# RWKV scan: b with U and k with V in opposite halves of the partitions, products over 128 rows, tokens turned 128 wide

## The reference, cut to what matters

```python
def rwkv7_scan(r, w_log, k, v, kk, a, s0):
    def step(s, inp):
        r_t, wl_t, k_t, v_t, kk_t, a_t = inp
        s = (s * jnp.exp(wl_t)[:, :, None, :]
             - jnp.einsum('bhvk,bhk->bhv', s, kk_t)[..., None] * (kk_t * a_t)[:, :, None, :]
             + v_t[..., None] * k_t[:, :, None, :])
        return s, jnp.einsum('bhvk,bhk->bhv', s, r_t)
```

## Time and profile before

| What | Value |
|---|---|
| Time, median of 3 runs | 4886.89 us (4883.68 to 4888.92) |
| The profiled execution's own time | 4901.24 us |
| Its span | 4899.6 us |
| Granted clock of PE over the span | 0.895 |
| PE busy, matmuls | 3998.6 us (82%) |
| DVE, ACT, POOL busy | 2176.6 (44%), 1063.4 (22%), 848.4 us (17%) |
| RWKV scan, from 1009 to 1618 us of the span | 609 us |
| PE busy in the scan | 444.58 us |

### The profile page before, as it was taken

The page is one execution under the profiler, slowest core; times in us unless marked ns, Lnnn a source line. Parts: engine busy times, 40 slices in busy tenths (PEclk is TensorE's granted clock), DMA queues, the critical chain, the costliest instruction groups (busy, mean ns, idle before and its releaser), DMA issues. The chain is left out here.

```text
span 4899.6 us, 92546 instructions
## 1 busy us (share of the span) xinstructions
PE 3998.6 (82%) x37777; PEld 3630.9 (74%) x37777; DVE 2176.6 (44%) x3758; ACT 1063.4 (22%) x1753; POOL 848.4 (17%) x636
## 2 busy tenths in 40 slices
PE   6999676357777788468999999899398289999998
PEld 4999232156666677158999999799377189999998
DVE  3333334233333354245655565500354437555555
ACT  3111233612222343222200010201243313010001
POOL 2222000000000332020222222122011111222221
PEclk8999888679888899679999999999677599999999
DMA  3222555321111221221111111122133411111111
GB/s 128 91 91 73 184 200 174 143 71 52 44 55 42 79 71 53 101 64 31 37 48 43 38 37 41 55 86 79 39 113 100 134 33 40 40 38 44 47 43 60
DMA packets 439455, 360.46 MB, mean 74 GB/s; under 512 B 63220, under 2 KB 417709, under 8 KB 436621
## 3 DMA queue, kind: packets, MB, share of 16 engines
q1 hardware_dynamic: 427729, 287.07, 19.3%
q0 software_dynamic: 10304, 60.98, 3.1%
q10 hardware_dynamic: 1152, 8.39, 0.4%
HBM read 270.45 MB, written 85.92 MB: 73 GB/s over the span
## 5 line engine op out<-in xcount | busy, mean ns | idle before, releaser
L91 POOL TENSOR_TENSOR ffn_w_lower<-ffn_w,ffn_w_upper 128x1024 fp32r<-128x1024 f32 x164 | 393.2, 2398 | 1359.1 <-DVE ffn_w_upper L86 1359.1
L931 DVE SCALAR_TENSOR_TENSOR rstd<-u_tile,ffn_taps,rstd 128x945 f32<-128x945 f32 (+3 forms) x440 | 490.6, 1115 | 85.2 <-ACT rstd L878 71.3
L99 PE MATMUL ffn_ps<-HU,ffn_w_upper 128*128 128x384 f32 x2112 | 481.9, 335 | 29.0 <-DVE ffn_w_lower L91 25.7
L99 PE MATMUL ffn_ps<-HL,ffn_w_upper 128*128 128x384 f32 x2112 | 481.1, 335 | 0.0
L99 PE MATMUL ffn_ps<-HU,ffn_w_lower 128*128 128x384 f32 x2112 | 480.7, 335 | 0.0
L99 PEld LDWEIGHTS ffn_ps<-HU,ffn_w_upper 128*128 128x128 f32 x2112 | 377.1, 188 | 31.8 <-issue 29.2
L99 PEld LDWEIGHTS ffn_ps<-HL,ffn_w_upper 128*128 128x128 f32 x2112 | 377.9, 189 | 0.0
L99 PEld LDWEIGHTS ffn_ps<-HU,ffn_w_lower 128*128 128x128 f32 x2112 | 377.8, 188 | 0.0
L99 PE MATMUL ffn_out_ps<-g_upper,ffn_w_upper 128*128 128x384 f32 x1056 | 355.5, 337 | 22.9 <-DVE g_lower L91 14.5
L99 PE MATMUL ffn_out_ps<-g_lower,ffn_w_upper 128*128 128x384 f32 x1056 | 354.4, 336 | 0.0
L99 PE MATMUL ffn_out_ps<-g_upper,ffn_w_lower 128*128 128x384 f32 x1056 | 354.4, 336 | 0.0
(11 more groups left out here) (468 smaller groups left out, 6588.3 us busy)
## 6 DMA issues: line engine op xcount, KB each, us to landing
ffn_w<-in_ffn_w_in_dram SPq DMA_DIRECT2D x88, 512.0 KB
ada_w<-in_ada_w_dram SPq DMA_DIRECT2D x40, 1024.0 KB, 6.1
rwkv_units<-unit_rows POOLq DMA_DIRECT2D x8, 2304.0 KB, 9.2
un<-rwkv_units SPq DMA_DIRECT2D x36, 512.0 KB, 4.3
z_even<-z_tile POOLq DMA_DIRECT2D x31, 576.0 KB, 3.1
in_w<-in_ab_w_in_dram SPq DMA_DIRECT2D x31, 512.0 KB
gun<-gdn_units SPq DMA_DIRECT2D x72, 192.0 KB, 3.6
z_odd<-z_tile POOLq DMA_DIRECT2D x24, 576.0 KB, 4.9
```

Source lines behind the costliest of these rows:

```text
L91: return eng.tensor_tensor(out.bitcast(F32R), x, up, ALU.subtract)
L99: mm = pe.matmul(o, w(a).bitcast(F32R), r.bitcast(F32R), start=(first and n == 0), stop=(last and n == 2))
L931: dve.scalar_tensor_tensor(out=o, in0=i, scalar=tp[:, t:t + 1], in1=o, op0=ALU.mult, op1=ALU.add).then_inc(s["conv"] if n < NCONV else s[" ...
```

## The change

Vectors b and k are now put so that for pairs with r = 0 b is `un[..., 2]` and k is `un[..., 3]`, and for r = 1 the other way round. With that:

- `products` takes both at once as one weight of 128 columns: 16 matmuls a step in place of 32, each 64 rows by 128 columns. `NA` then holds b's and k's products of one lane in opposite halves of the partitions.
- `bk_tokens` turns b and k of a pair in one transposition of 128 by 128 (8 a step), `v_tokens` turns v of two pairs in one (4 a step); before there were 32 and 16 products with an identity.
- The new tile `BK` holds b and k turned, `UV` holds U and V, U in the half of the partitions where b is and V where k is. So `update` and `out_own` sum over 128 rows in one matmul, 16 a step each in place of 32.
- ACT copies U into two halves (two instructions of 64 partitions in place of one of 128), V in two of 64 partitions and 512 columns in place of k's two of 128 and 256.
- `vv` swaps the two pairs of a group, so each load of it becomes two DMAs. `v_tokens` waits for ACT's first copy of `BK`, where `k_tokens` waited for the second of `BV`.
- In `rwkv_prep_phase` only the places of b and k within `un` change.

```diff
+        BK = sbuf(ctx, nc, "bk_tok", [P, 2, 4, 2, P])
+        UV = sbuf(ctx, nc, "uv_tok", [P, 2, 2, 2, 2, 2, 64])
...
-                            sp.dma_start(vv[:, k, d], v_src[c]).then_inc(loaded[k], 16)
+                            for r in range(2):
+                                sp.dma_start(vv[:, k, d, 1 - r::2], v_src[r][c]).then_inc(loaded[k], 16)
...
+                    def bk_tokens(step):
...
+                            for r in range(2):
+                                for d in range(2):
+                                    mm = pe.transpose(ps[:, g, 2, (2 * r + d) * P:(2 * r + d) * P + P],
+                                                      un[:, a // 2, d, 2 * g + r, 2:4, :].rearrange("p u t -> p (u t)"), K["ident"][:])
+                        pe_.did(mm, f"{a}bk")
...
-                                for h, r in QUARTERS:
-                                    u = un[HALF[h], a // 2, d, 2 * g + r]
-                                    o = w * 256 + d * P
-                                    mm = pe.matmul(ps[HALF[r], g, h, o:o + P], u[:, 2 + w, :], u[:, 0:2, :].rearrange("p u t -> p (u t)"),
-                                                   start=True, stop=True)
+                                for h in range(2):
+                                    u = un[HALF[h], a // 2, d, 2 * g + r].rearrange("p u t -> p (u t)")
+                                    o = r * 256 + d * P
+                                    mm = pe.matmul(ps[:, g, h, o:o + P], u[:, 2 * RL:4 * RL], u[:, 0:2 * RL], start=True, stop=True)
...
-                            pe.matmul(o, BV[HALF[r], a // 2, h, g, 0, d, :], Ub[HALF[r], h, g, d, :], start=True, stop=False)
-                            mm = pe.matmul(o, KT[HALF[r], a // 2, h, g, d, :], BV[HALF[r], a // 2, h, g, 1, d, :],
-                                           start=False, stop=True)
+                            mm = pe.matmul(o, BK[:, a // 2, 2 * g + r, d, h * 64:h * 64 + 64], UV[:, a // 2, r, g, d, h, :],
+                                           start=True, stop=True)
...
-                            pac.did(act.activation(Ub[:].rearrange("p h g d v -> p h (g d v)"), pq[:, :, 256:512], ACT.Copy),
-                                    f"{b}U")
+                            for r, x in enumerate(HALF):
+                                pac.did(act.activation(UV[x, b // 2, r].rearrange("p g d h v -> p h (g d) v"),
+                                                       pq[x, :, 256:512].rearrange("p h (x v) -> p h x v", v=64), ACT.Copy),
+                                        f"{b}U" if r else f"{b}U0")
```

More of the change, by code:

```diff
@@ L1637, in rwkv_scan_phase @@
             u_src = units.rearrange("q d p c u t -> d c p q (u t)")
-            v_src = zc[8:12].rearrange("q p (c t) -> c p q t", t=RL)
+            v_src = [zc[8 + r:12:2].rearrange("q p (c t) -> c p q t", t=RL) for r in range(2)]
             y_dst = yscan.rearrange("d q p (c t) -> d c p q t", t=RL)
@@ L1657, in sources @@
                     def sources(step):
-                        return [x for d in range(2) for x in (u_src[d, rwkv_chunk(step, d)], v_src[rwkv_chunk(step, d)])]
+                        return [x for d in range(2) for x in (u_src[d, rwkv_chunk(step, d)], *[v_src[r][rwkv_chunk(step, d)] for r in range(2)])]
                     def load(step):
@@ L1705, in first @@
                             o, u = (2 * g + d) * 64, un[HALF[h], a // 2, d, 2 * g + r]
-                            mm = pe.matmul(ps[HALF[r], h, 2, o:o + 64], u[:, 0, :], u[:, 2, :], start=True, stop=True)
+                            mm = pe.matmul(ps[HALF[r], h, 2, o:o + 64], u[:, 0, :], u[:, 2 + r, :], start=True, stop=True)
                         pe_.did(mm, f"{a}y0")
-                    def tokens(step):
+                    def bk_tokens(step):
                         it, a = step
@@ L1727, in products, with v_tokens @@
                         settle(pe, B)
-                        for w in range(2):
+                        for r in range(2):
                             for d in range(2):
-                                for h, r in QUARTERS:
-                                    u = un[HALF[h], a // 2, d, 2 * g + r]
-                                    o = w * 256 + d * P
-                                    mm = pe.matmul(ps[HALF[r], g, h, o:o + P], u[:, 2 + w, :], u[:, 0:2, :].rearrange("p u t -> p (u t)"),
-                                                   start=True, stop=True)
+                                for h in range(2):
+                                    u = un[HALF[h], a // 2, d, 2 * g + r].rearrange("p u t -> p (u t)")
+                                    o = r * 256 + d * P
+                                    mm = pe.matmul(ps[:, g, h, o:o + P], u[:, 2 * RL:4 * RL], u[:, 0:2 * RL], start=True, stop=True)
                         pe_.did(mm, f"{a + g}a")
-                    def k_tokens(step):
+                    def v_tokens(step):
                         it, a = step
-                        ac.wait(pe, f"{a}bv1", it)
+                        ac.wait(pe, f"{a}bk0", it)
                         settle(pe, B)
[L1741 to L1745, removed]
+                        for g in range(2):
+                            for d in range(2):
+                                mm = pe.transpose(ps[:, 0, 2, (2 * g + d) * P:(2 * g + d) * P + P],
+                                                  vv[:, a // 2, d, 2 * g:2 * g + 2, :].rearrange("p q t -> p (q t)"), K["ident"][:])
+                        pe_.did(mm, f"{a}v")
                     def lanes4(*units):
@@ L1771, in rhs_own @@
                             o = (2 * g + d) * 64
-                            mm = pe.matmul(pq[HALF[r], h, o:o + 64], NA[HALF[r], a + g, h, 1, d, 0, :], BV[HALF[r], a // 2, h, g, 1, d, :],
-                                           start=False, stop=(g, d) == (1, 1))
+                            mm = pe.matmul(pq[HALF[r], h, o:o + 64], NA[HALF[1 - r], a + g, h, r, d, 0, :],
+                                           UV[HALF[1 - r], a // 2, r, g, d, h, :], start=False, stop=(g, d) == (1, 1))
                         if g == 1:
@@ L1817, in out_own @@
                             o = pq[HALF[h], r, (2 * d + g) * 64:(2 * d + g) * 64 + 64]
-                            pe.matmul(o, Ub[HALF[r], h, g, d, :], NA[HALF[r], a + g, h, 0, d, 1, :], start=False, stop=False)
-                            mm = pe.matmul(o, BV[HALF[r], a // 2, h, g, 1, d, :], NA[HALF[r], a + g, h, 1, d, 1, :],
+                            mm = pe.matmul(o, UV[:, a // 2, r, g, d, h, :], NA[:, a + g, h, r, d, 1, :],
                                            start=False, stop=(g, d) == (1, 1))
@@ L1850, in slot @@
                             products(new, g)
-                        tokens(new)
+                        bk_tokens(new)
                         if old is not None:
                             solve(old)
-                        k_tokens(new)
+                        v_tokens(new)
                         for g in range(2):
                             dv.wait(pe, f"{a + g}n1", it)
-                        ac.wait(pe, f"{a}kt1", it)
+                        ac.wait(pe, f"{a}v1", it)
                         for l in range(1, NL - 1):
@@ L1893, in slot @@
                         it, a = new
[L1894 to L1897, removed]
+                        pe_.wait(act, f"{a}bk", it)
+                        for g in range(2):
+                            ac.did(act.activation(BK[:, a // 2, 2 * g:2 * g + 2].rearrange("p r d c -> p (r d c)"), ps[:, g, 2, :],
+                                                  ACT.Copy), f"{a}bk{g}")
                         if old is not None:
                             solved()
[L1900 to L1903, removed]
+                        pe_.wait(act, f"{a}v", it)
+                        for r, x in enumerate(HALF):
+                            ac.did(act.activation(UV[x, a // 2, 1 - r].rearrange("p g d h v -> p (g d h v)"), ps[x, 0, 2, :], ACT.Copy),
+                                   f"{a}v{r}")
                         levels(1, 2, 3)
```

25 lines of the change are left out of this document (8 added, 17 removed).

## The result

The changed kernel takes 4864.44 us (median of 8, 4852.98 to 4877.73) beside 4887.91 us for the kernel before: a ratio of 0.9948, interval 0.9929 to 0.9968, 23 us faster. The forecast was 4837 us, 50 us faster; the time is inside the range, but the gain is less than half of the one forecast.

The account below looks back on a forecast made before the run. The prediction took the arrival of PE's instruction blocks to bound the scan: 9.0 + 35.35 + 12.8 + 5.25 = 62.4 us a pass in place of 67.97, 49.9 us over the scan, so 4837 us, range 4765 to 4905.

Parts of the forecast that it names:

- late code: Scan loop: PE executes most instruction blocks quicker than the next arrives; stops of 15.86 us in a 67.97 us pass.
- 1280 loads and 11 packets a pass: Scan loop: weight loads fall from 1640 to 1280 a pass, so instruction blocks from 14 to 11.
- The 0.17 us ahead of `update`: Levels 1 and 3: expected sign of the changes of shape, 0.17 us of "issue" before and behind `update` and `out_own`.
- Rival A: Scan loop: code alone sets the pace, 10.9 blocks at 4.86 us, 53.1 us a pass, 4754 us; chance 0.18.
- B: Scan steps: ACT's added copies and half-clock changes of shape outweigh fewer stops, +28 us over the scan, 4915 us; chance 0.14.
- C: Scan levels: waits for DVE and ACT replace the stops, no net change within 0.2%, 4887 us; chance 0.11.
- the straight steps hold the same work; scaled over the scan: Steps outside the loop: gain like the loop's, so 5.57 us a pass times 8.96 passes gives 49.9 us.
- the price of a block: Within the loop's levels: each of seven blocks takes 5.05 us whatever it holds, 35.35 us a pass.
- how the blocks were counted: Loop pass: a new block every 117 loads, counted from the top of the pass, 1640 loads over 14 packets.
- ACT's chain and the head's changes of shape: Step's head before level 1: six copies add 0.60 us, two changes of shape on the path 0.34 us.
- new changes of shape: Levels 1 and 3, around `update` and `out_own`: at most 1.0 us a step, costed at nothing under late code.
- The prediction's 34 us for eleven changes a step: Scan: by the skill's draining rule alone, eleven more changes of shape a step at 0.17 us, leaving no gain.

Follow-up runs that it names:

- shift 0 or 256: Changed kernel, or the one before, with no or 256 semaphore increments on PE ahead of the first step; passes 62.5 and 62.7 us changed, 67.7 and 67.3 before.
- the four places of each kernel: Kernel before with 0, 64, 112, 160 added increments, passes 67.7, 69.1, 68.4, 70.6 us; changed with 0, 60, 128, 200, passes 62.5, 67.8, 70.6, 66.1.
- the repeats': Changed kernel with empty PE instructions added that turned out not to be in what PE ran; ratios 0.9962 and 0.9959 to the kernel before.
- shift 200: Changed kernel with 200 semaphore increments on PE ahead of the first step, moving the loop's code; ratio 1.0058 to the kernel before, pass 66.1 us.
- V first: Changed kernel with V copied by DVE instead of ACT and `v_tokens` ahead of the old step's `solve` on PE; 4849.68 us, ratio 0.9931 to before.

## Why the prediction was wrong

Right: late code stops PE in the scan; 1280 loads and 11 packets a pass; PE's busy time stays; the loads of `vv` are free in the loop, where PE waits for no DMA. The 0.17 us ahead of `update` stood there before the change as well; behind it, where the prediction looked for another, the loads follow within 0.07 us. Rival A's 53 us a pass was never near. B's and C's mechanisms were both in part at work.

**The step at which the number failed is "the straight steps hold the same work; scaled over the scan".** The scan gained 24.4 us and not 49.9 (607.5 to 583.2). Of the 25.5 us that are missing the loop has 2.9 and the straight steps 22.6: they were to gain 10.9 and lost 11.7. Same work, other places. At shift 0 or 256 the head takes 94.8 us in the mean of four executions and took 91.1 in two, the end 46.1 and 42.0: 7.8 us lost where 11 were to be gained. Over the four places of each kernel head and end together take 137.1 us before and 138.1 changed, so some six packets fewer (27 and 21 at shift 0) brought these steps nothing. In the four straight steps the longer wait ahead of level 1 is 4.2 us of the loss. Another piece is one stop, a few loads behind the loop's exit (weight loads, changed kernel):

```profile
1543.77 0.24 PEld L1707 LDWEIGHTS scan_ps<-un 64*64 64x64 f32 x8 [0.63 <-issue]
1548.63 0.73 PEld L1707 LDWEIGHTS scan_ps<-un 64*64 64x64 f32 x24 [4.62 <-issue]
```

Before, the block there ended 65 loads on and not 8, and the stop was 2.01 us:

```profile
1575.89 0.96 PEld L1733 LDWEIGHTS scan_ps<-un 64*64 64x64 f32 x33
1578.86 0.20 PEld L1733 LDWEIGHTS scan_ps<-un 64*64 64x64 f32 x8 [2.01 <-issue]
```

**The second is the price of a block.** "5.05 us in the mean, and that does not depend on what the block holds": it does. The same 11 blocks of the same work took 62.4 or 66.1 us a pass, and 12 took 67.8 or 70.6, by where they end. In the pass shown above one end costs 3.03 us and another 0.78, and at the ends that lie 206 and 809 loads in, counted in steps of 120 from the stops, PE doesn't stop at all. Over the four places 0, 64, 112 and 160 the pass of before takes 68.9 us (67.5 as the mean of shifts 0 and 256, 69.1, 68.4, 70.6) with 14.25 blocks, or 4.84 each; over 0, 60, 128 and 200 the changed one takes 66.7 us (62.4 as the mean of four executions at shift 0 or 256, 67.8, 70.6, 66.1) with 11.5, or 5.8 each. So 2.75 blocks fewer came to 2.2 us a pass; by the forecast's price, 5.57 us for three blocks, they would be 5.1. The places lie up to 8 us apart, and with four of each the 2.2 has a standard error of 1.8 us: the mean worth is clear neither of nothing nor of 5.1. What is clear is that one price for every block doesn't hold. Over the scan the change's worth in the mean of the places is some 14 us (619.3 to 605.3, the means of the scans over the same places, the repeats' 579.4 and 575.2 among those at shift 0). Fewer blocks mean more work between two ends, and the time of a pass is work and waits plus the stops that nothing covers.

**The third is how the blocks were counted.** They were counted from the top of the pass, which for before was right by accident (0 to 5 into a block), and at 117 loads each, which was not: a pass brings 14 packets but is 13.5 blocks long (3451 instructions, 256 a block), so a block is 122 loads. Before's stops stand 368, 489, 610, 852 and so on loads into a pass, near multiples of 122; "Counting 117 loads from the top of the pass leads to each stop" misses them by 17 to 59 loads. The changed loop begins 72 to 77 instructions into a block. Nearest to the places that the sum assumed is shift 200 (16 to 21 in), and there a pass takes 66.1 us and not 62.4: the agreement of the loop with the forecast is a coincidence of a low price and a lucky place.

**Two terms were too small.** ACT's chain and the head's changes of shape, 0.94 us a step, measured 2.35 - 1.06 = 1.29 us of wait. And level 1 with its new changes of shape, costed at nothing under late code, takes 3.30 us at full clock (1303.33 to 1306.63, no stop for code inside) where before it took 2.87 (two rows of before, level 1 and the first of level 2):

```profile
1314.56 0.62 PEld L1439 LDWEIGHTS scan_ps<-Y,NA 64*64 64x64 f32 x32 [1.06 <-issue]
...
1317.43 0.13 PEld L1439 LDWEIGHTS scan_ps<-Y,NA 64*64 64x64 f32 x1
```

Before, seven steps of the loop have a level 1 with no stop for code inside, 2.84 to 3.06 us; the changed kernel's at full clock are 3.21 to 3.31, some 0.3 us more. The larger part is the clock, 1.3 us in 8 of 14 steps. The sum had nothing for that; rival B had the lower clock, but as a price of the changes of shape, and V first, with the same shapes and a short wait, shows full clock in all 14. What these terms cost a pass is not shown: V first took the wait and the lower clock back and gained nothing at its place, as the prediction's reason for costing them at nothing would have it.

By the Trainium skill ("TensorEngine Tiling (Array Packing)", section "Tiling Modes") a change of mode drains TensorE. The 0.3 us of level 1 agree with it, though no run here separated the shapes from the rest of that level. The prediction's 34 us for eleven changes a step, taken from the 49.9 us of its sum, would have left 16 us and not "nothing".

What stays open: why one end of a block costs nothing and another 3 us, and so the worth of the change at a place not tried; and whether the stages behind the scan, whose code moved too, gained or lost, since one and the same program began its scan anywhere from 990 to 1007 us.

## What to carry to other kernels

Where an engine stops with no releaser at an even distance of instructions, count the instructions from the program's start and not from the loop's, and price a stop at what it lasted, not at the distance between two: the 15.86 us of stops over 14 blocks would have forecast 3.4 us a pass for three blocks. Time a change of such a loop at a few shifts of the code, with a shift by one whole block as control: here the place was worth 8 us of a pass of 66.7, the change 2.2 with a standard error of 1.8. And look first at what the change puts on an engine that the bound one waits for: moving V's two copies gave 1.5 us a pass at one place and 2.3 at another, though it moved the code by two loads as well.

## What the runs showed of the hardware

- The same loop with the same 1280 loads took 62.3 to 70.6 us a pass as its code was moved by 0 to 200 instructions, and 62.7 us, nearly the old time, at 256.
- Behind the loop's exit PE stopped for 3.5 to 4.6 us where a block ended 8 loads on (the changed kernel, four executions), and for 2.0 and 2.3 us where it ended 65 loads on (before, shifts 0 and 256).
- Behind a wait of 2.14 us on PE, level 1 ran partly at the lower clock in 8 to 11 of the loop's 14 steps (the changed kernel, four executions); behind 0.95 us (before, shifts 0 and 256) or 0.70 us (V first) in none.
- Copies of 64 partitions by 512 columns took ACT 592 ns each, those of 128 by 512 595 ns; on DVE 689 ns.
